# A ninth slot for the gathered v rows, paid for with a norm weight that TensorE spreads

## The chip, the cores and the metric

The kernel runs on one core of one Trainium2 chip. The metric is the device time in microseconds from launch to end; lower is better. A core has TensorE (PE), VectorE (DVE), ScalarE (ACT), GpSimd (POOL) and the queue engine SyncE (SP), each with its own instruction stream, run in order, and 16 DMA engines that all queues share. SBUF and PSUM have 128 partitions.

## What is computed

One layer of a trunk over 1024 tokens of width 1024, in float32: a mixer (latent attention, a gated linear recurrence, differential attention), a cross attention to 256 memory tokens, and an expert layer, then a last norm. The part that moves most bytes is the expert layer. For every token it picks 128 of 16384 experts (8 heads, 16 each); every expert has a row `u` and a row `v` of 1024 numbers:

```python
def peer_ffn(h, w_q, keys, u, v):          # h = rmsnorm(x, norm_ffn)
    ...
    def block(args):
        xt, et, gt = args
        act = jax.nn.gelu(jnp.einsum('td,thkd->thk', xt, u[et]), approximate=False)
        return jnp.einsum('thk,thkd->td', gt * act, v[et])
```

## The kernel before, in words

The tokens go in 8 blocks of 128, one token to a partition. Each block has a front (norm, projections, both attentions, recurrence, cross attention, top-k of the experts) and then its expert rows. The expert rows of block b are worked off while the front of block b+1 runs, so that each engine's stream interleaves two things: pieces of the front, and "positions" p = 0 to 127 of the rows. Tables written out by hand (`TENSOR_STOPS`, `VECTOR_STOPS`, `SCALAR_STOPS`) say for each front piece up to which position the engine has to go before it runs that piece. After block 7's front only rows are left. Block 0's front has no rows beside it.

**Rows.** POOL gathers one row of `u` or `v` for each of the 128 tokens with one indirect DMA of 512 KB (`gather_u`, line 792; `gather_v`, line 802). Its order is fixed: u row i, then v row i-12 (`GATHER_LAG`), then u row i+1, and so on. Both kinds have a ring of `G_RING` = 8 slots, and before each gather POOL waits until the slot's last row was used, so that one gather that has to wait holds up all behind it. DVE multiplies u row p with the normed tokens `h_cur` (line 1986) and counts `u_used`. ACT and DVE turn the products into coefficients; ACT writes them to a diagonal (line 1466). Of v rows, PE multiplies seven of eight with that diagonal and sums in the PSUM tile `ps_sum` (line 1212, 13 positions behind, `v_used`); every eighth (`on_vector`) is added by DVE into `x_cur` (line 2007, `v_added`). Row j lies in slot j % 8, so the DVE's rows always use slot 7, and counters `SUM_SLOTS` = 7 and one credit of `v_added` stand for the free slots of the two readers.

With eight slots, v row i-12 waits for v row i-20, which PE reaches at its position i-7; u row i waits for u row i-8, at DVE's position i-8.

**The norm of the experts.** At the end of a block's front `hand_ids` (line 1950) makes `h_cur` out of `x_next`, the row's scale and the weights `norm_ffn`. The weights lie in SBUF as `ffn_row`, 128 equal copies of one line of 1024 numbers (4 KB of each partition), loaded once at the start by a DMA of 512 KB, the last of the constants on SP's queue.

**The score banks.** `ps_s` is a PSUM tile of two banks that many pieces share. In `peer_scores` PE writes two sets of key scores to it, and ACT copies each out (line 1252, `k_out`) before the next may be written. From there until `latents` of the following block nobody uses `ps_s`.

## Time and profile before

| | |
|---|---|
| median of 3 runs | 3508.47 us (3501.45 to 3508.81) |
| the profiled execution, its own time | 3502.22 us |
| its span, first to last instruction | 3500.1 us |
| PE, DVE, ACT, POOL busy | 84%, 67%, 23%, 57% |
| mean rate of DMA over the span | 385 GB/s |
| span of block 0's front without rows | about 0 to 313 us |
| last block, rows only | about 3152 us to the end |

Busy time of an engine is a share of the whole span; waits are put down to what ended them. "DMA busy" of a stretch is the mean over the 16 engines. A PE in this profile is busy from issue to a modelled end, and one float32 matmul is listed as two instructions.

### The profile page before, as it was taken

To read this page: it belongs to the slowest core of one execution; us is meant where nothing else is said; L and a number is where in the kernel's file an instruction comes from. 1 tells how busy PE (TensorE), PEld (TensorE's weight loads), DVE (VectorE), ACT (ScalarE), POOL (GpSimd) and SP (SyncE) were. 2 spreads that over 40 slices of the span, in tenths; PEclk is the share of its full clock that TensorE was granted. 3 is DMA by queue.
4 is the path that set the end of the run, shared out by engine and by line. 5 is a ranking of instruction groups with operands and counts; after the bars stand their busy time and mean duration, and the time that the engine had idled before them with its cause. 6 is when DMAs were issued, how large, how long until landed. Compare 5 with 4: busy or idle time off the path is not lost.

```text
span 3500.1 us, 34723 instructions
## 1 busy us (share of the span) xinstructions
PE 2942.9 (84%) x10960; PEld 1660.0 (47%) x10960; DVE 2341.0 (67%) x5884; ACT 814.6 (23%) x1924; POOL 2008.2 (57%) x2085
## 2 busy tenths in 40 slices
PE   7786898888997899888987799888998789976777
PEld 6465355533554355444554445544554445522222
DVE  6229756886578765887477855786648866596554
ACT  3111421133111422133211332114221232211111
POOL 1003765666565664666555655666547655577775
PEclk9897999999999999999999999999999999998999
DMA  7787999999999999999999999999999999999998
GB/s 275 259 299 266 409 409 409 408 409 402 409 402 408 399 405 403 407 409 390 405 409 408 397 351 409 409 408 370 354 409 409 409 346 350 390 404 410 409 409 339
DMA packets 387256, 1346.12 MB, mean 385 GB/s; under 512 B 41793, under 2 KB 44865, under 8 KB 386433
## 3 DMA queue, kind: packets, MB, share of 16 engines
q0 software_dynamic: 294912, 1073.87, 78.0%
q1 hardware_dynamic: 91008, 265.83, 20.1%
q10 hardware_dynamic: 1152, 4.19, 0.3%
q8 instruction: 89, 1.46, 0.2%
q14 instruction: 95, 0.77, 0.1%
HBM read 1334.03 MB, written 35.39 MB: 391 GB/s over the span
## 4 chain that ended last, share of the span: by engine, by line
PE 43%; DMA 25%; DVE 14%; POOL 9%; issue 6%; ACT 3%; SPq 0%; DVEq 0%; ACTq 0%; POOLq 0%
PE ps_sum L1212 19%; DMA rows<-in_peer_u,ids_u 9%; PE ps_p L979 7%; DMA rows<-in_peer_v,ids_v 6%; DMA rows<-in_peer_v,ids_u 5%; POOL rows L802 5%; PE ps_s L1127 5%; POOL rows L792 4%; DVE rows L1986 4%; DMA w_ring<-packed 2%; PE ps_s L1065 2%; PE ps_p L1073 2%; DVE feat_b L1873 1%; PE ps_p L1047 1%; DVE feat_b L1869 1%
## 5 line engine op out<-in xcount | busy, mean ns | idle before, releaser
L1212 PE MATMUL ps_sum<-rows,diag 128*128 128x512 f32 x3584 | 1748.0, 631 | 271.9 <-DMA rows<-in_peer_v,ids_v 129.2
L1986 DVE CUSTOM_DVE_ANT_0 rows<-h_cur,rows 128x1024 f32<-128x1024 f32 x1024 | 1228.1, 1220 | 539.7 <-DMA rows<-in_peer_u,ids_u 527.0
L792 POOL DMA_INDIRECT rows<-in_peer_u,ids_u x1024 | 1005.4, 982 | 720.7 <-issue 498.8
L1212 PEld LDWEIGHTS ps_sum<-rows,diag 128*128 128x128 f32 x3584 | 684.1, 201 | 1166.4 <-issue 1047.8
L802 POOL DMA_INDIRECT rows<-in_peer_v,ids_v x512 | 493.5, 964 | 452.2 <-PE ps_sum L1212 295.6
L802 POOL DMA_INDIRECT rows<-in_peer_v,ids_u x512 | 494.4, 966 | 267.8 <-issue 127.3
L1466 ACT ACTIVATE diag<-ident,acts 128x128 f32<-128x128 f32 x896 | 327.4, 394 | 1057.4 <-PE ps_sum L1212 757.5
L979 PE MATMUL ps_p<-hT,w_ring 128*128 128x128 f32 x2944 | 367.8, 286 | 36.1 <-DMA w_ring<-packed 18.0
L979 PEld LDWEIGHTS ps_p<-hT,w_ring 128*128 128x128 f32 x2944 | 362.0, 202 | 68.6 <-issue 42.3
L1772 DVE CUSTOM_DVE_ANT_0 e<-ps_s,bias_t 128x256 f32<-128x256 f32 (+6 forms) x96 | 74.2, 773 | 177.5 <-PE ps_s L1065 70.6
L2007 DVE SCALAR_TENSOR_TENSOR x_cur<-rows,acts,x_cur 128x1024 f32<-128x1024 f32 x128 | 164.0, 1282 | 13.4 <-DMA rows<-in_peer_v,ids_v 13.4
L1843 DVE TENSOR_TENSOR x_next<-x_next,ps_s 128x512 f32<-128x512 f32 x32 | 21.9, 685 | 189.8 <-PE ps_s L1127 189.8
L1454 ACT ACTIVATE acts<-dots 128x8 f32<-128x8 f32 x128 | 26.6, 207 | 453.2 <-DVE dots L1986 453.0
L1127 PE MATMUL ps_s<-w_ring,hT 128*128 128x512 f32 x256 | 117.7, 606 | 12.7 <-DVE hT L1833 6.8
L1379 ACT ACTIVATE e<-e,small 128x256 f32<-128x256 f32 (+6 forms) x96 | 75.4, 786 | 220.6 <-DVE small L1774 220.2
L979 PE MATMUL ps_p<-pT,w_ring 128*128 128x128 f32 x1024 | 118.6, 276 | 1.2 <-DMA w_ring<-packed 0.6
L979 PEld LDWEIGHTS ps_p<-pT,w_ring 128*128 128x128 f32 x1024 | 116.8, 192 | 5.6 <-issue 3.3
L1127 PE MATMUL ps_s<-w_ring,feat_b 128*128 128x512 f32 x256 | 115.4, 594 | 1.1 <-ACT feat_b L1252 0.7
L1065 PE MATMUL ps_s<-k_diff,feat_a 32*128 32x512 f32 (+2 forms) x192 | 84.2, 545 | 24.9 <-DVE small L1774 24.7
L1873 DVE FIND_INDEX8 feat_b<-feat_b,e 128x8 uint32<-128x128 f32 (+1 forms) x384 | 103.4, 279 | 0.0
L1252 ACT ACTIVATE feat_a<-ps_p 128x512 f32<-128x512 f32 (+2 forms) x48 | 26.0, 541 | 317.5 <-PE ps_p L979 317.4
L1986 DVE DVE_READ_ACCUMULATOR2_ANT dots<- 128x1 f32 x1024 | 84.5, 83 | 0.0
(280 smaller groups left out, 2325.7 us busy)
## 6 DMA issues: line engine op xcount, KB each, us to landing
w_ring<-packed SPq DMA_DIRECT2D x343, 512.0 KB, 7.7
w_ring<-in_wstream SPq DMA_DIRECT2D x65, 512.0 KB, 5.3
packed<-in_wstream SPq DMA_DIRECT2D x49, 512.0 KB, 7.9
rows<-in_peer_u,ids_u POOLq DMA_INDIRECT x1024, 13.3
rows<-in_peer_v,ids_u POOLq DMA_INDIRECT x512, 10.7
rows<-in_peer_v,ids_v POOLq DMA_INDIRECT x512, 15.4
bias_rows<-rows SPq DMA_DIRECT2D x5, 1024.0 KB, 12.8
bias_t<-in_x SPq DMA_DIRECT2D x8, 512.0 KB, 6.2
```

The lines of the kernel that those rows point to most:

```text
L792: pool.indirect_dma_start(u_rows[:, j % G_RING, :], None, peer_u, bass.IndirectOffsetOnAxis(ap=ids_u[:, j:j + 1], axis=0)).then_inc(u_land ...
L802: pool.indirect_dma_start(v_rows[:, j % G_RING, :], None, peer_v, bass.IndirectOffsetOnAxis(ap=ids[:, j:j + 1], axis=0)).then_inc(v_landed ...
L979: ins = pe.matmul(dst, w[:, k, :], lhs[:, kt, :], start=(kt == 0), stop=(kt == KT - 1))
L1065: ins = pe.matmul(ps_s[:, c0:c1], q_diff[r:r + DK, half // 4, :], k_diff[r:r + DK, half // 4, c0:c1], start=True, stop=True)
L1127: pe.matmul(ps_s[:, n * 512:(n + 1) * 512], lhs[:, kt, :], w, start=(kt == 0), stop=(kt == KT - 1)).then_inc(w_used, 1)
L1212: ins = pe.matmul(ps_sum[:, c * 512:(c + 1) * 512], diag[:, n % 4, :], v_rows[:, j % G_RING, c * 512:(c + 1) * 512], start=(n == 0), stop= ...
L1379: act.activation(buf[:, 0:keys_n], buf[:, 0:keys_n], ACT.Exp, bias=small[:, 32 + n:33 + n], accum_out=small[:, 48 + n:49 + n]).then_inc(s_ ...
L1466: act.activation(diag[:, n % 4, :], ident[:, :], ACT.Copy, scale=coef[:, j:j + 1]).then_inc(diag_made, 1)
L1772: run(dve.tensor_tensor_reduce(buf[:, 0:keys_n], ps_s[:, 0:keys_n], bias[:, 0:keys_n], 1.0, -3.0e38, ALU.add, ALU.max, small[:, 16 + n:17 ...
L1873: dve.max_index(i[:, first:first + 8], v[:, first:first + 8], s).then_inc(top_step, 1)
L1986: dve.tensor_tensor_reduce(row, h_cur[:, :], row, 1.0, 0.0, ALU.mult, ALU.add, dots[:, p:p + 1]).then_inc(u_used, 1)
L2007: dve.scalar_tensor_tensor(x_cur[:, :], v_rows[:, j % G_RING, :], coef[:, j:j + 1], x_cur[:, :], ALU.mult, ALU.add)\
```

## The change

The ring of v rows gets a ninth slot; that of u rows keeps eight. Rows of all blocks are counted through, and v row j of block b lies in slot (128 b + j) % 9. So the slot of a DVE row moves around the ring, and `gather_v` waits for whoever used the row nine before, by a count that is computed for each row. The slot takes the 4 KB of each partition that `ffn_row` had. The weights are now one line of 4 KB in partition 96 under `k_mla`, which uses partitions 0 to 95, and `spread_ffn` lets PE multiply it with a line of ones into `ps_s`, two matmuls per block of one row of weights by 512 columns each. It runs at the start of the piece `next_norm` in blocks 0 to 6 and right behind `peer_scores` in block 7. PE waits for ACT's second copy out of `ps_s` before it, DVE waits for it in `hand_ids` and reads the weights from PSUM, and `latents` of the next block waits until DVE has read them. The order of the pieces and the stops are the same.

```diff
-G_RING = 8
+U_RING = 8
+V_RING = 9
...
-SUM_SLOTS = G_RING - G_RING // SHARE
+SUM_SLOTS = 7
+ADD_SLOTS = 1
...
-        ffn_row = sb("ffn_row", [P, D])
...
-        k_mla = sb("k_mla", [NOPE + ROPE, MLA_H, SEQ])
+        k_lines = sb("k_lines", [P, MLA_H, SEQ])
+        k_mla = k_lines[0:NOPE + ROPE, :, :]
+        ffn_line = k_lines[96:97, 0, :]
...
-            sp.dma_start(ffn_row[:, :], ffn_gain.partition_broadcast(P)).then_inc(consts_in, 16)
+            sp.dma_start(ffn_line, ffn_gain.partition_broadcast(1)).then_inc(consts_in, 16)
...
+            def gather_v(b, j):
+
+                slot = row_slot(b, j, V_RING)
+                before = b * EXPERTS + j - V_RING
+                if before >= 0:
+                    added = before // SHARE + (1 if on_vector(before % EXPERTS) else 0)
+                    if on_vector(before % EXPERTS):
+                        pool.wait_ge(v_added, ADD_SLOTS + added)
+                    else:
+                        pool.wait_ge(v_used, SUM_SLOTS + before + 1 - added)
...
+            def spread_ffn(b):
+                if isinstance(b, int) and b == 0:
+                    pe.wait_ge(consts_in, 96)
+                pe.wait_ge(k_out, 2 * b + 2)
+                for c in range(2):
+                    ins = pe.matmul(ps_s[:, c * HALF:(c + 1) * HALF], ones[96:97, :], ffn_line[:, c * HALF:(c + 1) * HALF],
+                                    start=True, stop=True)
+                ins.then_inc(ffn_spread, 1)
+
+            def later_norm(b):
+                spread_ffn(b)
+                turn_scaled(b + 1)
+
+            def last_scores(b):
+                peer_scores(b)
+                spread_ffn(b)
+
             def latents(b):
                 pe.wait_ge(lat_sq, b + 1)
+                ge(pe, handed, b)
...
+                dve.wait_ge(ffn_spread, b + 1)
-                dve.scalar_tensor_tensor(h_cur[:, :], x_next[:, :], small[:, 105:106], ffn_row[:, :], ALU.mult, ALU.mult)\
+                dve.scalar_tensor_tensor(h_cur[:, :], x_next[:, :], small[:, 105:106], ps_s[:, :], ALU.mult, ALU.mult)\
                    .then_inc(handed, 1)
```

## Rows read from the trace of the kernel before

**Rows 1.** page, slices of 87.5 us: mean DMA busy tenths, GB/s moved.

```profile
DMA  7787999999999999999999999999999999999998
GB/s 275 259 299 266 409 409 409 408 409 402 409 402 408 399 405 403 407 409 390 405 409 408 397 351 409 409 408 370 354 409 409 409 346 350 390 404 410 409 409 339
```

**Rows 2.** page, DMA queues: packets, MB, share of 16 engines.

```profile
q0 software_dynamic: 294912, 1073.87, 78.0%
```

**Rows 3.** page, groups: busy us, mean ns of one | idle before, releaser.

```profile
L1212 PE MATMUL ps_sum<-rows,diag 128*128 128x512 f32 x3584 | 1748.0, 631 | 271.9 <-DMA rows<-in_peer_v,ids_v 129.2
L1986 DVE CUSTOM_DVE_ANT_0 rows<-h_cur,rows 128x1024 f32<-128x1024 f32 x1024 | 1228.1, 1220 | 539.7 <-DMA rows<-in_peer_u,ids_u 527.0
L792 POOL DMA_INDIRECT rows<-in_peer_u,ids_u x1024 | 1005.4, 982 | 720.7 <-issue 498.8
...
L802 POOL DMA_INDIRECT rows<-in_peer_v,ids_v x512 | 493.5, 964 | 452.2 <-PE ps_sum L1212 295.6
```

**Rows 4.** waits of the whole run: us, times, longest.

```profile
POOL rows L802 <- PE ps_sum L1212: 419.5, 209, 13.3
...
POOL rows L792 <- DVE dots L1986: 221.6, 171, 20.8
```

**Rows 5.** stretches: length, busy us of PE, PEld, DVE, ACT, POOL, clock, DMA, GB/s.

```profile
811.00:823.00 12.00, 12.00 (x35) 5.33 (x33) 5.38 (x16) 5.11 (x11) 8.52 (x10) 0.99 0.97 360
...
989.00:999.00 10.00, 10.00 (x25) 4.46 (x24) 9.71 (x47) 2.05 (x7) 7.52 (x9) 1.00 0.97 358
...
1213.00:1253.00 40.00, 39.02 (x124) 18.50 (x123) 31.27 (x82) 17.47 (x40) 28.47 (x30) 1.00 1.01 386
...
1391.00:1401.00 10.00, 10.00 (x24) 4.37 (x23) 9.72 (x50) 2.00 (x6) 7.56 (x9) 1.00 0.98 351
...
1609.00:1679.00 70.00, 66.03 (x207) 32.66 (x206) 43.22 (x102) 23.90 (x53) 43.19 (x44) 1.00 1.00 380
...
2005.00:2081.00 76.00, 70.86 (x235) 36.83 (x236) 47.97 (x108) 26.73 (x55) 44.99 (x47) 0.96 0.91 330
...
2411.00:2513.00 102.00, 94.40 (x318) 49.09 (x319) 60.67 (x130) 35.27 (x69) 54.91 (x56) 0.97 0.91 328
...
2829.00:2941.00 112.00, 101.72 (x349) 52.44 (x348) 65.79 (x136) 37.85 (x70) 55.71 (x58) 0.97 0.87 314
...
3049.00:3063.00 14.00, 13.68 (x36) 6.95 (x37) 12.23 (x58) 4.09 (x10) 7.85 (x9) 1.00 0.82 286
```

**Rows 6.** waits within 2829 to 2941 us.

```profile
POOL rows L802 <- PE ps_sum L1212: 29.4, 12, 5.9
```

**Rows 7.** timeline of POOL: start, us, instruction [idle before <- releaser].

```profile
2087.20 0.94 POOL L792 DMA_INDIRECT rows<-in_peer_u,ids_u  x1 [7.97 <-DVE dots L1986]
...
2506.99 0.93 POOL L792 DMA_INDIRECT rows<-in_peer_u,ids_u  x1 [8.00 <-DVE dots L1986]
```

**Rows 8.** one microsecond of the stretch after 2506.99, columns of rows 5.

```profile
2510.00:2511.00 1.00, 1.00 (x4) 0.53 (x3) 0.00 (x0) 0.00 (x0) 0.69 (x2) 1.00 0.75 291
```

**Rows 9.** timeline of the last block's PE, ACT and POOL.

```profile
3049.32 1.97 PE L1182 MATMUL ps_s<-keys,feat_a 128*128 128x256 f32 x8 [1.36 <-ACT e L1252]
3051.12 17.33 PE L1212 MATMUL ps_sum<-rows,diag 128*128 128x512 f32 x40
...
3051.33 1.11 ACT L1252 ACTIVATE e<-ps_s,small 128x1024 f32<-128x1024 f32 x1 [2.15 <-PE ps_s L1182]
...
3053.28 0.94 POOL L802 DMA_INDIRECT rows<-in_peer_v,ids_v  x1 [3.93 <-PE ps_sum L1212]
```

**Rows 10.** timeline of PE, same place one of the earlier blocks.

```profile
1006.41 1.97 PE L956 MATMUL ps_p<-ident,feat_a 128*128 128x128 f32 x8 [3.91 <-DVE feat_a L1662]
```

**Rows 11.** groups of DVE: one reading no PSUM, one reading PSUM.

```profile
L1950 DVE SCALAR_TENSOR_TENSOR h_cur<-x_next,small,ffn_row 128x1024 f32<-128x1024 f32 x8 | 10.3, 1285 | 0.0
...
L2025 DVE TENSOR_TENSOR x_cur<-x_cur,ps_sum 128x1024 f32<-128x1024 f32 x1 | 1.2, 1221 | 2.9 <-PE ps_sum L1212 2.9
```

**Rows 12.** chain that ended last, first 40 us: start, us, what.

```profile
15.59 7.90 DMA w_ring<-in_wstream
```

More of the change, by code:

```diff
@@ L292, in sem @@
             return ctx.enter_context(nc.semaphore(name))
-        rows = sb("rows", [P, 2 * G_RING, D])
-        u_rows, v_rows = rows[:, 0:G_RING, :], rows[:, G_RING:2 * G_RING, :]
+        rows = sb("rows", [P, U_RING + V_RING, D])
+        u_rows, v_rows = rows[:, 0:U_RING, :], rows[:, U_RING:U_RING + V_RING, :]
         w_ring = sb("w_ring", [P, W_RING, 2 * HALF])
@@ L434, in program @@
         x_copied, gain_landed = sem("x_copied"), sem("gain_landed")
+        ffn_spread = sem("ffn_spread")
         x_handed, ids_handed, v_ids_handed = sem("x_handed"), sem("ids_handed"), sem("v_ids_handed")
-        u_landed = [sem(f"u_landed{i}") for i in range(G_RING)]
-        v_landed = [sem(f"v_landed{i}") for i in range(G_RING)]
+        u_landed = [sem(f"u_landed{i}") for i in range(U_RING)]
+        v_landed = [sem(f"v_landed{i}") for i in range(V_RING)]
         u_used, v_used = sem("u_used"), sem("v_used")
@@ L545, in row_of, with row_slot, row_landings @@
             return (bp, None) if isinstance(bp, int) and bp == 0 else (bp - 1, j + EXPERTS)
+        def row_slot(b, j, ring):
+            return (b * EXPERTS + j) % ring
+        def row_landings(b, j, ring):
+            return 16 * ((b * EXPERTS + j) // ring + 1)
         def ends_block(bp, p, at):
@@ L891, in _ @@
             for k in range(GATHER_LAG):
-                gather_u(k)
+                gather_u(0, k)
             for b in range(NB):
-                retrieve(more=b < NB - 1)
+                retrieve(b, more=b < NB - 1)
         @block.tensor
@@ L1195, in _ @@
                 front[f"next_{g}"] = lambda b, g=g, first=first, n=n: project(b + 1, g, first, n)
-            front["next_norm"] = lambda b: turn_scaled(b + 1)
+            front["next_norm"] = later_norm
             for h in range(4):
@@ L1206, in add_row @@
                     pe.wait_ge(diag_made, bp * SUM_ROWS + n + 1)
-                    pe.wait_ge(v_landed[j % G_RING], bp * (16 * EXPERTS // G_RING) + 16 * (j // G_RING + 1))
+                    slot = row_slot(bp, j, V_RING)
+                    pe.wait_ge(v_landed[slot], row_landings(bp, j, V_RING))
                     if j == 0:
@@ L1211, in add_row @@
                     for c in range(2):
[L1212 removed]
+                        ins = pe.matmul(ps_sum[:, c * 512:(c + 1) * 512], diag[:, n % 4, :], v_rows[:, slot, c * 512:(c + 1) * 512],
                                         start=(n == 0), stop=(n == SUM_ROWS - 1), skip_group_check=True)
@@ L1239, in _ @@
             for pace.body, (first, last, wide[0]) in enumerate(LOOPS):
+                if first == NB - 1:
+                    front["peer_scores"] = last_scores
                 with pe.Fori(first, last) as b:
@@ L1982, in multiply_row @@
             def multiply_row(bp, p):
-                dve.wait_ge(u_landed[p % G_RING], bp * (16 * EXPERTS // G_RING) + 16 * (p // G_RING + 1))
-                row = u_rows[:, p % G_RING, :]
+                slot = row_slot(bp, p, U_RING)
+                dve.wait_ge(u_landed[slot], row_landings(bp, p, U_RING))
+                row = u_rows[:, slot, :]
                 dve.tensor_tensor_reduce(row, h_cur[:, :], row, 1.0, 0.0, ALU.mult, ALU.add, dots[:, p:p + 1]).then_inc(u_used, 1)
@@ L2001, in position @@
                 if j is not None and on_vector(j):
-                    dve.wait_ge(v_landed[j % G_RING], at * (16 * EXPERTS // G_RING) + 16 * (j // G_RING + 1))
-                    dve.wait_ge(v_added, at * (EXPERTS // SHARE) + (j + G_RING) // SHARE)
+                    slot = row_slot(at, j, V_RING)
+                    dve.wait_ge(v_landed[slot], row_landings(at, j, V_RING))
+                    dve.wait_ge(v_added, at * (EXPERTS // SHARE) + j // SHARE + ADD_SLOTS)
                     dve.wait_ge(coef_made, at * STEPS + (j // STEP + 1))
-                    dve.scalar_tensor_tensor(x_cur[:, :], v_rows[:, j % G_RING, :], coef[:, j:j + 1], x_cur[:, :], ALU.mult, ALU.add)\
+                    dve.scalar_tensor_tensor(x_cur[:, :], v_rows[:, slot, :], coef[:, j:j + 1], x_cur[:, :], ALU.mult, ALU.add)\
                        .then_inc(v_added, 1)
```

41 lines of the change are left out of this document (18 added, 23 removed).

## The prediction, as it was put on record

> **What bounds the kernel now.** I read the page's slices first. From 350 us on the DMA row stands at 9 in every slice but the last, which is an 8, and most slices move 409 GB/s; several move less, down to 346 [rows 1]. So 409 GB/s is the full rate here. 2048 gathers move 1073.87 MB [rows 2], 0.524 MB each, which at 409 GB/s is 1.28 us, and a pair (one u, one v) is 2.56 us. The groups say the same from the other side: DVE's u rows wait 527 us for their gathers, PE's v rows 129 us for one of their two kinds alone [rows 3]. The kernel is bound by DMA wherever the rate is 409, and a change that leaves the bytes alone can only win back time in which the rate is lower. (409 less the rate) / 409 times 87.5 us, added over the 36 slices from 350 us on, is 94 us; 15 us of it are the last slice, where at last nothing is left to load. So 79 us are open.
>
> Next, who holds the gathers up. POOL waits 419.5 us for PE's use of v rows and 221.6 us for DVE's use of u rows [rows 4]. Most of that is harmless, because gathers already issued keep the queues full. It costs only where they run out, so I cut the run into stretches by rate [rows 5]. The loss of each is its length times its shortfall: 1.4 us (811), 1.3 (989), 2.3 (1213), 1.4 (1391), 5.0 (1609), 14.7 (2005), 20.2 (2411), 26.0 (2829), 4.2 (3049). That is 76.5 us, so these nine stretches hold nearly all of it. PE is busy for 91 to 100% of each. In the three wide ones (blocks with many key tiles) PE is busy 93%, 93% and 91%, and the largest wait of POOL is for PE's v rows, 29.4 us within 2829 to 2941 [rows 6].
>
> **The change part by part.**
>
> The ninth slot. POOL may now issue v row i-12 when PE is through position i-8, where it had to be through i-7. POOL therefore runs at most one pair ahead of where it ran: a credit of 2.56 us of DMA work, paid once each time the queues would run dry, if u's ring lets the u row through. It is not paid per wait. Where PE is the limit for a whole stretch, PE's end does not move: the DMA idles a pair less and that is kept only if DMA is the limit again before the next thing that holds POOL. So:
>
> - Short, light stretches (811, 989, 1213, 1391): each loses less than a pair, and rows wait for DMA soon after. All of it is won: 1.4 + 1.3 + 2.3 + 1.4 = 6.4 us. Bounds 3 us (a v slot alone, 1.28 us at most for each, some not kept) and 6.4.
> - 1609, 2005, 2411, 2829: behind each comes a wait of POOL for DVE's u rows, 7.97 and 8.00 us long in two of them [rows 7]. A ninth v slot does nothing there, since u's ring is as it was: POOL stands at the same u row until the same moment. If the queues empty meanwhile, the credit is gone. At 2510 us, behind the wait that ended at 2506.99, the rate is 291 GB/s [rows 8], so the queues had run thin there. I take 1 us each for 1609 and 2005, 0 for the other two; bounds 0 and 2.56 each, 0 to 10.2 in all.
> - 3049, in the last block: below.
>
> The Trainium skill ("Perfetto Trace Analysis", section Optimization Strategy) says that a gap that repeats on the engine that ought to be full can mean too few buffers for the next tile. By that rule all 76.5 us would be the ring's to give back; the trace agrees that the gaps repeat, but not that they are of one kind, since PE is the busy engine in the long ones [rows 5].
>
> The spread. Two matmuls of 512 columns are four listed instructions; v rows of the same columns run at 17.33 / 40 = 0.43 us each [rows 9], so 1.74 us of PE a block. Matmuls with a single row of weights are not in the trace; bounds are 1.0 us (four at 1.97 / 8 = 0.25 us, of half the columns [rows 9]) and 2.5 us (four at the page's mean of 631 ns [rows 3]); 0.43 us is nearest, being of the same columns and type and back to back. In blocks 0 to 6 it stands at `next_norm`, position 93, long after ACT's copy, and v rows wait behind it on PE. Its cover is PE's wait for DVE's scaled x, 3.91 us before the transposes at 1006.41 [rows 10]; the v rows between are 1.74 us late, less than the new lead of a pair. I take 0; without the cover it is 1.74 us in each.
>
> In block 7 there is no cover. It follows `peer_scores` at once, and must wait for ACT's copy, which runs from 3051.33 for 1.11 us, to 3052.44. Before, PE started v rows at 3051.12 [rows 9], and POOL, 3.93 us in waiting, issued its next v gather at 3053.28, on the first of them. Now v rows start at 3052.44 + 1.74 = 3054.2, so 3.1 us late, and POOL's lead is 2.56 us. The two cancel: +0.5 us. Bounds: -2.6 (the spread hides) and +3.1.
>
> DVE reads the weights from PSUM in `hand_ids`: 1285 ns now without a PSUM source, and 1221 ns for an add of the same size with one [rows 11]. Nothing, within 0.1 us eight times. The Trainium skill ("Perfetto Trace Analysis", section Optimizing Scalar/DVE Operations) gives some 125 ns of access overhead for PSUM against 60 for SBUF, an estimate of 0.5 us over the eight; the rows show none of it, and the sum would be -8.4 us by it. The new waits: DVE's for the spread comes some 30 positions after it; PE's in `latents` is covered by its wait for squares that DVE makes only behind `hand_ids`. Both 0. The u rows, the POOL instruction count and the gathers' order are unchanged: 0.
>
> The load. 512 KB become 4 KB, 1.28 us less on SP's queue, ahead of the fifth weight load, whose 7.90 us are in the chain of waits [rows 12]. Block 0 has no gathers to hide it. I take 1.0 us; bounds 0 and 1.3.
>
> Sum: -6.4 - 2.0 + 0.5 - 1.0 = -8.9 us. The profiled execution took 3502.22 us itself (span 3500.1), so 3493.3 us. The shown median is 3508.47, 6 us above that execution; a saving of waits is the same from either, so the predicted median is 3499.6 us.
>
> **The rivals.**
>
> *Every bubble pays.* The stretches are not one bound each: the wide ones have full patches inside, and where the queues fill up again between two PE pieces the pair is credited anew. With a full pair in 1609, 2005, 2411, 2829 and 3049, and two to three in the wide ones, that is 6.4 + 2 x 2.56 + 3 x 2.5 x 2.56 + 1.3 = 32 us at most, 3476; with one in each, 6.4 + 5 x 2.56 + 1.3 = 20.5 us, 3488. For it: several POOL waits for PE in each, 12 in the last [rows 6]. Against it: PE is busy above 90% there, and the waits for DVE behind. The rule of the Trainium skill on repeating gaps ("Perfetto Trace Analysis", Optimization Strategy) speaks for this rival.
>
> *Nothing is kept.* DVE's u ring holds POOL next, and the pair only moves the dry spot: 0 to -3 us, 3505 to 3508. For it: 221.6 us of waits for DVE [rows 4] that nothing here touches, and the lead needs a u row through as well. Against it: rows wait for DMA directly behind the light stretches.
>
> *The spread decides, slower.* If PE is what POOL waits for with dry queues when the spread comes, all of it is on the path: 7 x 1.74 + 3.1 = 15.3 us, less 2 us of start and light stretches, 3522. It decides once the v rows behind the spread come more than a pair, 2.56 us, late. That holds in block 7 (3.1 us); in the others only if the spread costs near its upper bound and something else is late as well, such as DVE's scaled x, so that PE's 3.91 us are gone.
>
> **How the numbers follow.** My forecast (4 to 13 us less) 0.53; every bubble pays 0.17; nothing is kept 0.20; the spread decides 0.10. Time 3499.6 us. The range must leave out two tenths at most: down to half of the first rival, 3485, and up past the second, to 3511; the forecast's own range is 3495 to 3504. 0.2% is 7 us, about what a measurement of this kernel can tell from none. Faster by more: six tenths of the forecast and all of the first rival, 0.50. Within: the rest of the forecast and most of the second, 0.40. Slower: 0.10.
>
> **What would show it.** Right: POOL's wait for PE's v rows falls well below 419.5 us; stretches below 409 GB/s vanish in the light blocks and stay in the wide ones, followed by the same 8 us for DVE; two matmuls into `ps_s` before the last block's v rows with some 1.3 us of wait for ACT; the other seven with no wait for ACT and PE still idle before the transposes behind them; the bytes less by 0.52 MB. It would be wrong if the wide stretches' losses of 61 us fall by more than a quarter, if a v row late behind the spread shows up as a dry queue in each block, or if DVE comes to wait more for u rows than now because v gathers stand ahead of them.

## The result, and the profile after

| | before | after |
|---|---|---|
| median of 20 runs | 3501.48 us | 3509.51 us |
| lowest to highest | 3495.92 to 3508.81 | 3501.32 to 3515.65 |
| the profiled execution's own time, span | 3502.22, 3500.1 | 3510.99, 3509.1 |
| DMA bytes | 1346.12 MB | 1345.62 MB |

The ratio is 1.0017 (95% interval 1.0009 to 1.0024): 6 us slower by the ratio and 8 by the medians, where the prediction had 9 us faster. That is inside the 0.2% that I had called no change, but on the other side of zero. In a second comparison (below) the ratio was 1.0005 (0.9996 to 1.0013), which isn't clear of no change. Slower by 2 to 8 us is the reading, and the 9 us that were forecast are out of reach of both intervals.

From the page of the changed kernel: the slices of GB/s, and the groups of v rows, u rows and gathers (they answer to [rows 1, 3]):

```profile
GB/s 268 266 291 275 409 409 409 408 409 406 409 406 408 382 405 409 409 409 372 391 409 408 408 344 410 409 409 377 347 409 409 409 343 351 382 403 397 410 409 346
...
L1249 PE MATMUL ps_sum<-rows,diag 128*128 128x512 f32 x3584 | 1750.2, 631 | 288.5 <-DMA rows<-in_peer_v,ids_v 144.7
L2027 DVE CUSTOM_DVE_ANT_0 rows<-h_cur,rows 128x1024 f32<-128x1024 f32 x1024 | 1228.7, 1221 | 550.7 <-DMA rows<-in_peer_u,ids_u 538.6
L805 POOL DMA_INDIRECT rows<-in_peer_u,ids_u x1024 | 1013.9, 990 | 860.2 <-issue 486.2
...
L819 POOL DMA_INDIRECT rows<-in_peer_v,ids_v x512 | 490.6, 958 | 355.5 <-PE ps_sum L1249 229.6
```

POOL's waits in the changed kernel (they answer to [rows 4]):

```profile
POOL rows L805 <- DVE dots L2027: 374.0, 206, 21.4
POOL rows L819 <- PE ps_sum L1249: 306.8, 207, 11.1
```

What the reader is to see: the forecast of one view came true, POOL waits less for PE (419.5 to 306.8 us). But it waits as much more for DVE (221.6 to 374.0), and DVE in its turn waits no less for its u rows (527.0 us before, 538.6 now). The hold went from one ring to the other.

The page also has the median time of a gather from its issue to its landing (last number). Before:

```profile
rows<-in_peer_u,ids_u POOLq DMA_INDIRECT x1024, 13.3
...
rows<-in_peer_v,ids_v POOLq DMA_INDIRECT x512, 15.4
```

and after:

```profile
rows<-in_peer_u,ids_u POOLq DMA_INDIRECT x1024, 13.9
...
rows<-in_peer_v,ids_v POOLq DMA_INDIRECT x512, 18.0
```

A v gather may now be issued up to 2.56 us earlier, and half of them (those by `ids_v`) take 2.6 us longer to land; the other half takes 0.6 us longer (10.7 to 11.3), and so do the u gathers. For the first half, then, the lead went into waiting between issue and landing. This repeats in the experiments below, on the chips of 3503 to 3507 us: 17.8 to 18.2 us in all eight profiles with nine v and eight u slots, 15.3 to 16.4 in all four with eight and eight, and for u rows 13.7 to 13.9 against 12.9 to 13.3.

Next, the blocks. DVE makes `h_cur` once a block, so I cut both runs at its starts; the columns are those of [rows 5]. Blocks 2, 3, 4 and the last stretch before the final `h_cur`, of the kernel before:

```profile
701.50:1102.70 401.20, 347.25 (x1293) 193.96 (x1292) 284.45 (x725) 97.25 (x239) 248.61 (x256) 0.94 1.02 406
1102.70:1506.00 403.30, 351.62 (x1317) 198.23 (x1316) 286.95 (x725) 99.26 (x239) 247.39 (x256) 0.95 1.02 405
1506.00:1908.60 402.60, 351.10 (x1365) 202.08 (x1364) 288.33 (x725) 102.27 (x239) 251.17 (x256) 0.97 1.02 404
2741.20:3151.50 410.30, 348.87 (x1171) 181.16 (x1170) 291.31 (x712) 106.89 (x234) 247.59 (x255) 0.96 0.97 378
```

and of the changed kernel:

```profile
700.50:1101.60 401.10, 345.86 (x1297) 193.12 (x1296) 284.37 (x724) 97.53 (x239) 251.33 (x256) 0.95 1.03 408
1101.60:1504.70 403.10, 355.43 (x1321) 198.42 (x1320) 286.72 (x724) 99.61 (x239) 250.13 (x256) 0.94 1.02 402
1504.70:1914.20 409.50, 361.19 (x1369) 207.34 (x1368) 288.33 (x725) 102.69 (x239) 248.04 (x256) 0.95 1.01 397
2746.20:3162.10 415.90, 353.79 (x1176) 183.82 (x1174) 291.88 (x713) 106.90 (x234) 250.56 (x256) 0.95 0.97 376
```

The first `h_cur` starts at 311.9 us (313.3 before) and the changed kernel is 1.0 to 1.4 us ahead up to 1504.7. Blocks 2 and 3 are 401.1 and 403.1 us long, and were 401.2 and 403.3: nothing was won there. Nearly the whole loss lies in block 4 (402.6 to 409.5) and in the last stretch (410.3 to 415.9).

Within blocks 2 to 4 of the changed kernel, the same stretches as in [rows 5]:

```profile
810.00:822.00 12.00, 12.00 (x36) 5.48 (x35) 5.33 (x16) 5.07 (x11) 8.67 (x10) 1.00 1.02 405
988.00:998.00 10.00, 10.00 (x24) 4.15 (x23) 9.72 (x47) 1.82 (x6) 7.56 (x9) 1.00 1.01 395
1180.00:1230.00 50.00, 44.26 (x140) 21.54 (x138) 31.33 (x68) 19.08 (x47) 32.65 (x35) 0.86 0.98 367
1390.00:1400.00 10.00, 10.00 (x24) 4.05 (x23) 9.72 (x49) 2.11 (x6) 7.50 (x8) 1.00 1.03 408
1590.00:1600.00 10.00, 9.75 (x27) 5.68 (x27) 6.01 (x13) 4.74 (x9) 7.13 (x9) 0.66 1.03 409
```

and of the kernel before, the two that answer to 1180 and to 1590:

```profile
1182.00:1232.00 50.00, 44.28 (x144) 21.60 (x142) 34.32 (x74) 19.39 (x47) 33.64 (x36) 0.93 1.01 392
1591.00:1601.00 10.00, 9.31 (x35) 5.13 (x36) 8.39 (x17) 5.72 (x11) 7.30 (x9) 1.00 1.02 406
```

811, 989 and 1391 are full now (losses 0.1, 0.3 and 0.0 us, by the method of the prediction). But 1180 to 1230 loses 50 x 42 / 409 = 5.1 us where the kernel before lost 50 x 17 / 409 = 2.1. Sum of the four: 5.6 us, and it was 6.2 to 6.4. The 1213 stretch itself (1211 to 1251 here) moves 370 GB/s for 386, so it did not fill. In block 4 the clock was granted at 0.66 from 1590 to 1600 us, where the kernel before had it whole, and the rate over the 20 us behind it is 357 for 395. The wide stretches, cut at the same distance from `h_cur` (2010 to 2086, 2418 to 2520, 2834 to 2946), lose 10.6, 18.5 and 26.6 us (14.7, 20.2 and 26.0 before), and the one of 1609 (1608 to 1678 here) loses 9.9 for 5.0.

The last block's PE, and POOL's next v gather behind it (they answer to [rows 9]):

```profile
3054.77 1.97 PE L1218 MATMUL ps_s<-keys,feat_a 128*128 128x256 f32 x8 [1.36 <-ACT e L1291]
3057.94 2.62 PE L1024 MATMUL ps_s<-k_lines,ones 1*128 1x512 f32 x4 [1.20 <-ACT e L1291]
3060.48 15.86 PE L1249 MATMUL ps_sum<-rows,diag 128*128 128x512 f32 x30
```

```profile
3064.54 0.94 POOL L819 DMA_INDIRECT rows<-in_peer_v,ids_v  x1 [9.76 <-PE ps_sum L1249]
```

From the second scores to the v rows it is 60.48 - 54.77 = 5.71 us, and was 51.12 - 49.32 = 1.80 [rows 9]: 3.9 us late. POOL stands 9.76 us, and stood 3.93. A timeline row of POOL in block 5 shows what became of the wait of 7.97 us [rows 7]:

```profile
2092.05 0.94 POOL L805 DMA_INDIRECT rows<-in_peer_u,ids_u  x1 [9.17 <-DVE dots L2027]
```

### The profile page after: what moved, and what is told of

It is laid out like the page before. It is cut to its first block, busy times and chain, and to the rows that moved or that the text cites. A ratio compares the mean times of both kernels' runs of the same rounds, so it can differ in the third digit from the quotient of the medians.

```text
span 3509.1 us, 34795 instructions
## 1 busy us (share of the span) xinstructions
PE 2958.0 (84%) x10992; PEld 1663.2 (47%) x10992; DVE 2342.0 (67%) x5884; ACT 816.8 (23%) x1924; POOL 2024.2 (58%) x2085
## 2 busy tenths in 40 slices
DMA packets 387114, 1345.62 MB, mean 383 GB/s; under 512 B 41777, under 2 KB 44849, under 8 KB 386290
## 4 chain that ended last, share of the span: by engine, by line
PE 39%; DMA 29%; DVE 13%; POOL 9%; issue 6%; ACT 3%; SPq 0%; DVEq 0%; ACTq 0%
PE ps_sum L1249 18%; DMA rows<-in_peer_u,ids_u 14%; DMA rows<-in_peer_v,ids_v 7%; PE ps_p L996 6%; POOL rows L805 5%; POOL rows L819 5%; PE ps_s L1163 4%; DMA rows<-in_peer_v,ids_u 4%; DVE rows L2027 4%; DMA w_ring<-packed 2%; PE ps_s L1101 2%; PE ps_p L1109 2%; DVE feat_b L1912 1%; PE ps_p L1083 1%; PE ps_s L1097 1%
## 5 line engine op out<-in xcount | busy, mean ns | idle before, releaser
L1249 PE MATMUL ps_sum<-rows,diag 128*128 128x512 f32 x3584 | 1750.2, 631 | 288.5 <-DMA rows<-in_peer_v,ids_v 144.7
L2027 DVE CUSTOM_DVE_ANT_0 rows<-h_cur,rows 128x1024 f32<-128x1024 f32 x1024 | 1228.7, 1221 | 550.7 <-DMA rows<-in_peer_u,ids_u 538.6
L819 POOL DMA_INDIRECT rows<-in_peer_v,ids_u x512 | 504.8, 986 | 216.5 <-issue 137.2
L2049 DVE SCALAR_TENSOR_TENSOR x_cur<-rows,acts,x_cur 128x1024 f32<-128x1024 f32 x128 | 164.1, 1282 | 13.9 <-DMA rows<-in_peer_v,ids_v 13.9
L1493 ACT ACTIVATE acts<-dots 128x8 f32<-128x8 f32 x128 | 26.6, 208 | 469.2 <-DVE dots L2027 469.0
## 6 DMA issues: line engine op xcount, KB each, us to landing
rows<-in_peer_u,ids_u POOLq DMA_INDIRECT x1024, 13.9
rows<-in_peer_v,ids_u POOLq DMA_INDIRECT x512, 11.3
```

The source lines that it names most:

```text
L819: pool.indirect_dma_start(v_rows[:, slot, :], None, peer_v, bass.IndirectOffsetOnAxis(ap=ids[:, j:j + 1], axis=0)).then_inc(v_landed[slot] ...
L1249: ins = pe.matmul(ps_sum[:, c * 512:(c + 1) * 512], diag[:, n % 4, :], v_rows[:, slot, c * 512:(c + 1) * 512], start=(n == 0), stop=(n == ...
L2027: dve.tensor_tensor_reduce(row, h_cur[:, :], row, 1.0, 0.0, ALU.mult, ALU.add, dots[:, p:p + 1]).then_inc(u_used, 1)
L2049: dve.scalar_tensor_tensor(x_cur[:, :], v_rows[:, slot, :], coef[:, j:j + 1], x_cur[:, :], ALU.mult, ALU.add)\
```

## The experiments

Times are given as the ratio to the kernel before in runs on the same chip. The chips differ: the kernel before took 3503 to 3507 us on the two of the runs e1 to e4, f and g, and 3730 (e5 to e8) and 3715 us (h) on the two others. The slots are for u and v rows; "early" is the last block's spread at position 89 as in the change, "late" is at 93.

| run | slots u, v | last spread | ratio | interval |
|---|---|---|---|---|
| the change | 8, 9 | early | 1.0017 | 1.0009 to 1.0024 |
| e1_spread_only | 8, 8 | early | 1.0013 | 1.0002 to 1.0025 |
| e2_ring_only | 8, 9 | none | 1.0009 | 0.9997 to 1.0020 |
| e3_late_spread | 8, 9 | late | 0.9992 | 0.9979 to 1.0006 |
| e4_spread_in_wait | 8, 9 | late, others moved | 1.0010 | 0.9999 to 1.0021 |
| f1_eight_late | 8, 8 | late | 0.9991 | 0.9980 to 1.0002 |
| f2_full_rows | 8, 9 | early, 128 rows | 1.0004 | 0.9993 to 1.0015 |
| f3_changed_again | 8, 9 | early | 1.0005 | 0.9996 to 1.0013 |
| f4_nine_late | 8, 9 | late | 1.0000 | 0.9990 to 1.0010 |
| g1_nine_nine | 9, 9 | late | 0.9958 | 0.9944 to 0.9971 |
| g2_nine_u | 9, 8 | late | 0.9972 | 0.9959 to 0.9984 |
| g3_eight_late | 8, 8 | late | 0.9981 | 0.9970 to 0.9991 |
| g4_nine_late | 8, 9 | late | 0.9991 | 0.9980 to 1.0002 |
| on the chips of 3715 to 3730 us | | | | |
| e5_eight_late | 8, 8 | late | 0.9982 | 0.9946 to 1.0017 |
| e6_full_rows | 8, 9 | early, 128 rows | 1.0150 | 1.0100 to 1.0199 |
| e7_nine_u | 9, 8 | late | 1.0048 | 1.0017 to 1.0078 |
| e8_late_again | 8, 9 | late | 1.0141 | 1.0092 to 1.0189 |
| h1_nine_u | 9, 8 | late | 1.0043 | 1.0019 to 1.0067 |
| h2_nine_u_early | 9, 8 | early | 1.0064 | 1.0035 to 1.0093 |

### The two halves of the change apart

The spread without the slot:

```diff
-V_RING = 9
+V_RING = 8
```

> Eight slots for v rows again; the line, its spread by TensorE and the load of 4 KB stay. Theory A, the spread is what costs: in the last block v rows come 3.3 us late without a slot's lead to cover it, elsewhere 2.6 us of PE seven times is partly on the path; the ratio to the kernel before is 1.002 or more (+8 us or more), and the ring had only given back 1 to 6 us of it. Theory B, the ninth slot is what costs (POOL's hold passes from PE's v rows to DVE's u rows): the spread costs its 3.3 us in the last block less 1 us of the smaller load, +1 to +3 us, ratio 1.0003 to 1.0009. In the profile: A sees shortfalls of the rate near positions 93 of each block that the kernel before has not; B sees them only in the last block.

The slot without the spread:

```diff
-            sp.dma_start(ffn_line, ffn_gain.partition_broadcast(1)).then_inc(consts_in, 16)
+            sp.dma_start(gain_row[:, :], ffn_gain.partition_broadcast(P)).then_inc(consts_in, 16)
...
-            sp.dma_start(gain_row[:, :], final_gain.partition_broadcast(P)).then_inc(gain_landed, 16)
+            sp.dma_start(ffn_line, final_gain.partition_broadcast(1)).then_inc(gain_landed, 16)
...
-                spread_ffn(b)
...
-                dve.wait_ge(ffn_spread, b + 1)
-                dve.scalar_tensor_tensor(h_cur[:, :], ..., ps_s[:, :], ALU.mult, ALU.mult)
+                dve.scalar_tensor_tensor(h_cur[:, :], ..., gain_row[:, :], ALU.mult, ALU.mult)
```

> Nine slots for v rows and no spread: the experts' weights lie spread over the partitions in the buffer of the final norm's weights, and the final norm is scaled by them too (this changes the output of the final norm); of the bytes, the 4 KB and the 512 KB loads change places. Theory A, the spread is what costs: the ring's saving is seen alone, 3 to 9 us below the kernel before, ratio 0.9975 to 0.999. Theory B, the ninth slot is what costs: 4 to 8 us above the kernel before, ratio 1.001 to 1.0023, with POOL's waits for DVE's u rows some 150 us more than before and those for PE 110 us less, and the fourth block (1475 to 1884 us) several us longer. Theory C, the ring is worth nothing and the two small costs of the spread add up: within 1 us of the kernel before.

Neither half is faster than the kernel before: +0.13% and +0.09% (the second interval reaches zero). The theories can't be told apart by these totals: the first interval holds both A and B, and of the second only A, the saving of 3 to 9 us, is outside. The executions of one kernel scatter by some 6 us either way; the profiles say more than the totals do, below.

### The last block

```diff
-                    front["peer_scores"] = last_scores
+                    front["top_0"] = spread_ffn        # with "top_0": (93,) in the last TENSOR_STOPS
```

> The changed kernel, but in the last block the spread stands four positions later, at position 93 in place of 89, when ACT's copy is done and v rows have been run. Theory A: the 3.3 us that v rows came late (and the fall of the clock behind them) are gone: 3 us less than the changed kernel, ratio to the kernel before about 1.0013. Theory B: the same 3 us at most, the rest of the loss stays, since it comes from the slot. A reading of no difference to the changed kernel would say that POOL's lead covered the late v rows.

The same kernel three times more:

> The nine-slot kernel with the spread of the last block at position 93 once more, to narrow its ratio (0.9992, 0.9979 to 1.0006 the first time). If the late v rows and the fall of the clock behind the early spread are the changed kernel's loss, it stands 5 to 9 us under the changed kernel again, at 0.998 to 1.000 of the kernel before; if the first reading was chance, at 1.001 to 1.002. In the profile, no fall of the clock within 10 us behind the last spread, and a loss under 3 us behind the last block's scores, where the changed kernel has 7.3.

> Nine slots and the late spread in the last block, beside the changed kernel on one chip. On a chip like the first: 5 to 9 us less than the changed kernel, 0.998 to 1.000 of the kernel before. On a chip like the second: the same as the changed kernel within 5 us, since there it is the slot that costs some 57 us.

> Eight u and nine v slots with the late spread: 0.999 to 1.001 of the kernel before on a chip like the first (0.9992 and 1.0000 so far), so 1 to 3 us above eight and eight, though the last block alone is 2.6 us better; 1.014 on a chip like the second. The prediction had 9 us less than eight slots.

And with eight slots for v rows (`V_RING = 8`), three times:

> Eight slots for v rows, the spread in the last block at position 93 (the pair to the run of late spread with nine slots, and to the run of spread only). So far the spread at 89 cost 5 to 8 us in the last block with either ring, of which 3.3 us are late v rows and the rest a fall of TensorE's clock right behind it. Theory 1, that is all there is to the loss: without it this kernel is within 2 us of the kernel before (ratio 0.9995 to 1.0005), and the last block's granted clock shows no fall within 10 us behind the spread. Theory 2, the spreads of the other blocks cost too: 3 us or more above the kernel before. What the nine-slot kernel with the late spread has less than this one is the ring's worth: 6 to 9 us by the prediction, 0 by the theory that the hold only passes to DVE's u rows.

> Eight slots and the spread of the last block at position 93 again: the last comparison fell on a chip on which the kernel before itself took 3730 us, with a longer tail of slow DMA packets (one in a hundred over 486 ns, against some 200 ns), so this one is for a chip like the first. If the chip is like the first: within 2 us of the kernel before by the theory that only the last block's spread costs; 3 us or more above it if the other spreads cost too. The nine-slot kernel of the same call less this one is the ring's worth: 0 by the theory of the hold that passes to DVE, 6 to 9 us less by the prediction.

> Eight and eight with the late spread, the third time: 0.9985 to 1.0 of the kernel before on any chip (0.9991 and 0.9982 so far), by the smaller load at the start and nothing else.

Then the spread early again, with 128 rows:

```diff
-                spread_ffn(b)
+                pe.wait_ge(k_out, 2 * b + 2)
+                for c in range(2):
+                    ins = pe.matmul(ps_s[:, c * HALF:(c + 1) * HALF], ones[:, :], mem_v[:, 0, c * HALF:(c + 1) * HALF],
+                                    start=True, stop=True)
+                ins.then_inc(ffn_spread, 1)
```

> The changed kernel with the spread of the last block at position 89 as it is, but its two matmuls read 128 rows (all ones times a part of the cross attention's values) in place of one, so the last block's u rows are multiplied by other weights than the reference's. Theory 1, matmuls of one row count as idle time for TensorE's clock: no fall of the clock directly behind it, each matmul takes some 433 ns like a v row's in place of 588, and the kernel is 2 to 4 us faster than the changed one (ratio to the kernel before 1.0005 to 1.001). Theory 2, it is the 1.2 us of waiting for ACT and the late rows that count: the clock falls here too, and the time is that of the changed kernel, ratio 1.0015 to 1.002.

> The changed kernel with 128 rows in place of one in the last block's two matmuls of the spread (so the last block's u rows meet other weights than the reference's) again. The theory that matmuls of one row count as idle time for the clock: no fall of the granted clock within 10 us behind them, as in its first run, and 2 to 4 us less than the changed kernel of this call. The theory that the wait and the late rows cost: the same time as the changed kernel.

The change itself again:

> The changed kernel itself again, beside the three variants on one chip. On a chip like the first: 1.001 to 1.0024 of the kernel before. If its last spread is the cause, the profile again has the clock at half for about 6.8 us from 1 to 2 us behind that spread and a loss of 6 to 10 us there; if the fall was chance, it is not there. The fourth block (seven us longer in the first profile, with three falls of the clock in its attention) tells whether that was chance: 402 us if so, 409 if not. On a chip like the second, both nine-slot variants took 1.5% more, and this one should too: 1.013 to 1.018.

The view that settles this block is the 25 us from the start of the second scores, one row for each kernel, columns as in [rows 5]. Before (eight slots, no spread):

```profile
3049.32:3074.32 25.00, 23.01 (x56) 10.36 (x56) 21.16 (x83) 5.92 (x14) 16.19 (x18) 1.00 0.91 340
```

The change (nine slots, early):

```profile
3054.77:3079.77 25.00, 23.80 (x51) 10.62 (x52) 17.71 (x78) 5.12 (x12) 11.43 (x14) 0.86 0.79 289
```

Spread only (eight slots, early):

```profile
3052.86:3077.86 25.00, 23.80 (x51) 10.64 (x52) 16.94 (x78) 5.11 (x12) 11.32 (x14) 0.86 0.66 244
```

Ring only (nine slots, no spread):

```profile
3058.35:3083.35 25.00, 24.52 (x60) 11.23 (x60) 22.45 (x85) 5.92 (x14) 16.23 (x18) 1.00 1.00 387
```

The first run with the late spread (nine slots):

```profile
3047.22:3072.22 25.00, 25.00 (x62) 11.58 (x63) 22.25 (x85) 5.92 (x14) 16.22 (x18) 1.00 1.00 383
```

The third run with eight slots and the late spread:

```profile
3053.45:3078.45 25.00, 24.67 (x60) 11.14 (x60) 21.64 (x84) 5.92 (x14) 16.16 (x17) 1.00 0.89 341
```

Nine slots, early, 128 rows (the f2 run):

```profile
3057.41:3082.41 25.00, 23.80 (x59) 11.20 (x60) 20.66 (x83) 5.92 (x14) 13.61 (x16) 1.00 0.88 328
```

Loss is 25 x (409 - rate) / 409 us:

| v slots | no spread | late | early, 128 rows | early |
|---|---|---|---|---|
| eight | 4.2 | 3.9, 4.2 | | 10.1 |
| nine | 1.3 | 1.6, 1.3, 2.0, 1.8 | 5.0 | 7.3, 7.6 |

Every cell fits a sum of three prices, to a few tenths. The slot gives 2.4 to 2.9 us (the pair was 2.56). The late spread costs nothing. The early one costs 5.8 to 6.0 us: 3.3 of it with 128 rows already, the late v rows. The other 2.5 come with the clock, 0.86 in all three early runs with one row and 1.00 in every other of the table.

A stretch that moves more bytes need not end sooner, so I took the time as well, from the start of the second scores to the block's `h_cur`: 102.2 to 103.0 us with eight v slots and no or a late spread, 99.5 to 100.8 with nine; early, 109.1 with eight and 107.0 and 107.3 with nine, and 104.3 with 128 rows. The differences are the same three prices: 2 to 3 us for the slot, none for the late spread, 6 to 7 for the early one, of which some 4 stay with 128 rows.

The totals are less clear. The f2 run was to be 2 to 4 us faster than the change on the same chip, and it is 1.0004 against 1.0005; the late spread with nine slots (f4) was to be 5 to 9 us faster, and it is 1.0000, some 2 us. So the price of the early spread, and the part of it that is clock, are read from this stretch alone and not confirmed by a total. On the slow chip e8_late_again, which was to lose under 3 us in the stretch, lost 5.5.

PE's rows of the f2 run, where the two matmuls stood in the same place behind the same wait for ACT:

```profile
3057.41 1.97 PE L1222 MATMUL ps_s<-keys,feat_a 128*128 128x256 f32 x8 [1.36 <-ACT e L1295]
3060.57 1.98 PE L1036 MATMUL ps_s<-mem_v,ones 128*128 128x512 f32 x4 [1.20 <-ACT e L1295]
3062.40 13.90 PE L1253 MATMUL ps_sum<-rows,diag 128*128 128x512 f32 x32
```

From the scores to the v rows 4.99 us, so 3.2 us late. Its clock was whole; in the change, it stood at half from 3059.2 us for 6.8 us, and again so, 1.3 us behind the spread's start, in the second profile of the change. So behind matmuls of one row beside a wait the clock fell, and behind those of 128 rows it did not. With one row this is three profiles of three on the chips of 3505 us, with 128 rows one, so it is likely rather than proven. On the chip of 3715 us the early one-row spread of h2_nine_u_early had no such fall, against what was expected of it; its v rows were 3.3 us late and its stretch lost 6.9 us, where the late spread of h1_nine_u lost 3.7. That is the price of late v rows without the clock's.

### The other seven spreads

The run of late spread, and `pace.part(0.6)` ahead of the spread in `later_norm` (position 99 for 93):

> As the run before it, and in the other seven blocks the spread stands directly ahead of the wait for DVE's scaled x (position 99 in place of 93), so it lies wholly in time in which PE waits. Theory A, the spread's 2.6 us of PE hold v rows up in each block: up to 7 times 1.7 to 2.6 us less than the run before it, so at or below the kernel before, ratio 0.996 to 1.000. Theory B, the slot costs: no difference to the run before it, within 1.5 us.

The change has the spread of block 2 and the transposes behind it so:

```profile
991.04 1.98 PE L1024 MATMUL ps_s<-k_lines,ones 1*128 1x512 f32 x4
992.95 10.57 PE L1249 MATMUL ps_sum<-rows,diag 128*128 128x512 f32 x24
1005.60 1.10 PE L973 MATMUL ps_p<-ident,feat_a 128*128 128x128 f32 x8 [2.09 <-DVE feat_a L1701]
```

The spread holds PE 1.91 us. PE's wait for DVE's scaled x is down from 3.91 us [rows 10] to 2.09, and the eight transposes take 1.10 us for 1.97, since the clock no longer falls there: in blocks 1 to 6 it fell to half at the transposes or within 1.5 us of their start in six of six before (in two only behind them), in none of six now. In the second profile of the change it fell in two of six, behind waits of 3.84 and 5.52 us. Moved into the wait, in block 5, the spread left this:

```profile
2217.03 1.98 PE L1025 MATMUL ps_s<-k_lines,ones 1*128 1x512 f32 x4
2220.62 1.93 PE L974 MATMUL ps_p<-ident,feat_a 128*128 128x128 f32 x8 [1.61 <-DVE feat_a L1701]
```

with this clock in the six microseconds at the transposes (columns as in [rows 5]):

```profile
2220.00:2226.00 6.00, 5.38 (x15) 3.39 (x16) 5.24 (x9) 0.40 (x1) 4.78 (x5) 0.72 1.03 410
```

where the run of late spread has

```profile
2221.00:2227.00 6.00, 5.56 (x19) 3.04 (x20) 5.46 (x9) 0.80 (x2) 4.70 (x5) 1.00 1.03 409
```

The clock fell so in five of the six blocks, with the wait itself down to 1.15 to 1.8 us in four of them: here, too, matmuls of one row next to a wait did not hold the clock up. It cost no length of a block, since the rate is 409 there, and the total (1.0010 against 0.9992) can't tell: the two intervals overlap. The theory that the seven spreads hold v rows up has nothing for it: out of their way, they gave no gain.

### Which ring

Nine slots for u rows and eight for v rows, with the late spread:

```diff
-U_RING = 8
-V_RING = 9
+U_RING = 9
+V_RING = 8
```

> The late spread with the ninth slot in the ring of u rows (nine for u, eight for v). Theory H, in the changed kernel POOL's hold passed from PE's v rows to DVE's u rows, so that either ring alone only moves it: POOL waits some 370 to 420 us for PE's v rows again and under 150 us for DVE's u rows, and the time is that of the eight-slot kernel with the late spread within 2 us. Theory U, the waits for DVE are the ones that end with dry queues in the wide stretches (2411, 2829): 3 to 8 us less than with eight and eight. The prediction's account (PE is the busy engine there) says no gain.

> Nine slots for u rows, eight for v rows, late spread. Theory P: no gain over eight and eight, one ring alone only moves the wait. Theory Q: no gain either; a loss on a chip like the second (1.0048 there). A gain of 3 us or more over eight and eight would say that u was the ring that mattered. POOL's waits for DVE's u rows should fall below 150 us and those for PE stay above 350.

> Nine u slots, eight v slots, the last block's spread at position 93, again. The theory that what is late is DVE's u row, so that only the ring of u pays: 0.996 to 0.9985 of the kernel before, DVE's waits for u rows near 480 us (before 527), and the first whole block some 3 us shorter. If the first reading was chance: 0.998 to 1.000, as eight and eight.

The same with the early spread:

> The changed kernel with its ninth slot in the other ring: nine u slots, eight v slots, the last block's spread at position 89. If slot and spread are separate costs: 5.8 us above the run before it, with a loss of about 10 us behind the last block's scores (that is the loss with eight v slots and the early spread; 7.5 with nine) and the clock at half for some 6.8 us there; ratio to the kernel before 0.998 to 1.000.

Nine in both rings; `gain_row` makes the room, and the final norm takes `mem_v[:, 0, :]` in its place:

> Nine slots in both rings, with the late spread; the room comes from the final norm's weights, which are left out (the final norm is scaled by a part of the cross attention's values instead, so its output differs, and 508 KB less are loaded, 1.2 us of DMA). Theory P, the lead needs a slot in both rings: the light stretches' 6.4 us and the wide ones' 2 us are won on top of the last block's 2.6, ratio 0.997 to 0.998. Theory Q, gathers in flight are not what the blocks wait for: no more than the 1.2 us of the load and the 2.6 us of the last block under eight and eight, ratio 0.998 to 1.0005 on a chip like the first, and more than 1.005 on a chip like the second.

On the chip of g1 to g4 the u slot is the one that pays: 0.9972, and with both 0.9958, of which 0.0004 is the load that is left out. Eight and eight with the late spread is at 0.9981 there, so most of 0.9972 is not the slot's: 3 us are by the ratios, 5 by the medians (3499.19 to 3494.39), from six executions of g2_nine_u; the two intervals overlap. On the two slower chips the same kernel lost (1.0048 and 1.0043), where 0.996 to 0.9985 had been expected of h1_nine_u. The waits of POOL and DVE in g2_nine_u:

```profile
POOL rows L820 <- PE ps_sum L1246: 496.6, 249, 12.9
...
POOL rows L806 <- DVE dots L2024: 120.5, 142, 19.5
```

```profile
DVE rows L2024 <- DMA rows<-in_peer_u,ids_u: 480.9, 309, 3.9
```

the same wait of DVE in g3_eight_late, the kernel with eight and eight on the same chip:

```profile
DVE rows L2024 <- DMA rows<-in_peer_u,ids_u: 510.6, 322, 4.2
```

and blocks 1 and 2 and the last stretch of g2_nine_u, cut at `h_cur`:

```profile
310.20:696.40 386.20, 324.16 (x1230) 186.99 (x1231) 274.70 (x710) 91.16 (x227) 240.67 (x250) 0.93 1.01 399
696.40:1097.70 401.30, 346.63 (x1296) 192.99 (x1295) 284.28 (x725) 97.61 (x239) 247.24 (x256) 0.95 1.02 405
...
2736.20:3143.10 406.90, 352.10 (x1176) 181.52 (x1174) 291.09 (x712) 106.66 (x234) 246.82 (x256) 0.96 0.98 383
```

POOL waits for PE longer than with eight and eight (496.6 us for 432.6 in g3_eight_late and 419.5 before the change), and the kernel is faster all the same. What fell is DVE's wait for u rows: 480.9 us, and 482.0 with nine and nine, where the four profiles with eight and eight have 501.8 to 527.0 and the eight with nine v slots 516.2 to 538.6. Block 1 is 386.2 us (385.6 with nine and nine), and 388.1 to 389.2 in the twelve profiles with eight u slots; the last stretch is 406.9, and was 410.3. Blocks 2 and 3 are 401.3 and 403.0: no ring shortened those, they sum to 803.4 to 804.5 us in all fourteen profiles.

The last row of the last block's table, for this kernel:

```profile
3040.23:3065.23 25.00, 24.39 (x59) 10.97 (x60) 23.10 (x88) 6.03 (x14) 16.17 (x17) 1.00 1.03 408
```

The rate is full, but from these scores to `h_cur` it takes 102.9 us, as with eight and eight: what this kernel gains in the last stretch lies ahead of the scores (304.1 us for 307.6 to 308.1 in three of the four profiles with eight and eight, 315.0 in the fourth).

## Why the prediction was wrong, by its steps

- **What bounds it.** Right in the large: most slices stay at 409 GB/s, and only time below that rate was open. The step that failed comes next: I took POOL's largest wait (419.5 us, for PE's v rows) as the one to shorten.
- **The ninth slot in the light stretches, -6.4 us.** This is the step that made the prediction wrong. Three of the four stretches did fill, as forecast (1213 did not: 370 GB/s for 386); the blocks did not get shorter (804.5 us before, 804.2 now, for blocks 2 and 3). I let the credit of a pair stand although POOL's next wait is for DVE, with the condition "if u's ring lets the u row through" in the text and no price on it. The rival that nothing is kept described it: the dry spot moved (5.6 us of loss for 6.4), and POOL's waits for DVE took over. The v gathers that were issued earlier took longer to land (15.4 to 18.0 us for half of them), and PE waited no less for them (129.2 to 144.7 us). That u rows are the ones that come late is argued from three things: DVE's 527 us stood beside PE's 129 in my own rows [rows 3] (53 more for PE's other kind), these waits fell with nine u slots, and block 1 got 2 to 3 us shorter with those alone. One of the signs that I had named for being wrong came: DVE waits more for u rows than before (538.6 us), but 11 us is within what kernels of the same rings differ by (501.8 to 527.0).
- **1609 and 2005, -1 us each.** Not won: the 1609 stretch loses more (9.9 us for 5.0), and the 2005 one less (10.6 for 14.7), but its block is 413.4 us for 412.1. 2411 and 2829, 0, were right. The waits for DVE behind 2005 and 2411 are 9.17 and 8.94 us (7.97 and 8.00 before).
- **The spread hidden in blocks 0 to 6.** Right: 1.91 us of PE (1.74 forecast), and the wait takes it.
- **The last block, +0.5 us.** Its mechanism was right and both its terms held: v rows 3.2 us late with the clock whole (3.1), the slot worth 2.6 (2.56). A third term was missing, 2.5 us of clock. Measured: 7.3 - 4.2 = +3.1, the upper bound.
- **`h_cur` from PSUM, 0.** Right; no access overhead of the order that the Trainium skill gives ("Perfetto Trace Analysis", section Optimizing Scalar/DVE Operations) can be seen. The group in the changed kernel, 1281 ns for 1285:

```profile
L1990 DVE SCALAR_TENSOR_TENSOR h_cur<-x_next,small,ps_s x8: 1276/1281/1281, 311.9 to 3162.1; 128x1024 f32<-128x1024 f32 x8
```

- **The load, -1.0 us (0 to -1.3).** Probably mis-sized. The first `h_cur` starts at 313.3 and 313.4 us in the two kernels that spread 512 KB at the start; in the twelve profiles with the line outside the slower chips at 307.6 to 313.6, mean 309.8. (The largest is a profile of the change itself, so one profile doesn't show it.) So it seems worth some 3.6 us, more than its own transfer; that is an estimate from two profiles against twelve that scatter by 6 us, and why it should be more was not tried. It agrees with eight slots and the late spread at 0.9991 and 0.9981.
- **Slower after all.** By these prices the change should come out at -3.6 + 3.1 = -0.5 us, and it was +8.0 and +1.8 (0.05%). So the slot for v rows may cost something beside its 2.6 us gain in the last block. The pairs on one chip point to how much: f4 less f1 is +0.0009, g4 less g3 +0.0010, 3 us each, and near 6 us with the last block's gain taken out; but in both pairs the intervals overlap. Whether and where it is lost isn't settled. A candidate is block 4, 6.9 us longer in the first profile with its clock at half from 1591 us on. Three of eight profiles with nine v slots show that (407.5 to 409.1 us from its first gather to the next block's; the other five 402.0 to 404.0), none of four with eight and eight does (401.6 to 403.5); the second profile of the change doesn't. But such long readings, most at a lower mean clock, come elsewhere and without the ninth slot too: block 6 takes 425.5 to 426.2 us (416.9 to 420.5 otherwise) in three profiles with nine v slots and in g3_eight_late, and the time from the last block's start to its second scores 314.4 to 316.3 us (304.1 to 311.2 otherwise) in three with nine and in e1_spread_only. Counted over these three places it is 9 of 24 readings with nine v slots, 2 of 12 with eight and eight, too few to tell. The same 2.24 us gap of PE stands ahead of it with and without the fall, so what decides is not in these rows.
- **The rival "the spread decides"** had the right sign, but by 7 x 1.74 us that were not on the path. Its deciding point, v rows more than 2.56 us late, was met in the last block alone (3.9 us there; the spread takes 1.91 us in the others).

The Trainium skill's rule on repeating gaps ("Perfetto Trace Analysis", Optimization Strategy: too few buffers for the next tile) is met in part: with nine u slots the runs on the chip of 3507 us agree with it, for 3 to 5 us of the 76.5; with nine v slots no run does, and on the slower chips neither ring does.

**Faster versions.** Nine u slots, eight v slots, the last spread late: 0.9972 of the kernel before on one chip, but 1.0048 and 1.0043 on the two chips of 3730 and 3715 us. Eight and eight with the late spread is below 1 on all three chips that ran it (0.9991, 0.9981, 0.9982), though only one interval stays clear of 1.

## What to carry to other kernels

The longest wait of the engine that issues transfers needn't name the ring that is too short. Ask which landed data an engine stands and waits for, and give the slot to that ring; if issue is in order, a slot elsewhere can just move the hold to the next instruction, and the lead into a longer time to landing. A dry stretch that fills is no gain until the next block boundary comes earlier: cut both traces there. And work placed on TensorE beside a wait should be priced with the clock behind it.

## What the runs showed of the hardware

- The clock fell behind matmuls of one row beside a wait as it did behind a wait: to half for 6.8 us in the last block of three profiles (not in h2_nine_u_early), and at the transposes in five of six blocks of e4_spread_in_wait. The two one-row matmuls took 1.91 us until the next work, the two of 128 rows 60.57 to 62.40, 1.83.
- Two of the four chips of the experiments ran the kernel before in 3730 and 3715 us. There the mean rate is lower in most slices. One in a hundred of the gathers' row packets took over 486 ns in e5_eight_late and 530 in e8_late_again, for 213 before and 199 after on the first chip. GB/s in slices, eight slots for v rows and then nine, both late:

```profile
GB/s 285 259 259 320 353 389 401 391 364 352 409 395 371 335 374 400 381 376 297 404 392 394 344 342 409 404 392 301 350 406 390 387 289 363 390 323 369 374 365 320
```

```profile
GB/s 275 263 254 316 347 381 382 397 347 338 406 387 369 346 364 400 373 363 324 394 391 381 333 317 396 386 382 325 329 398 394 368 289 339 370 339 361 367 377 312
```

There a ninth v slot costs 1.0141 - 0.9982, 1.6%, a ninth u slot 0.7% on that chip, and on the other its kernel is 0.4% above the kernel before. More slots and slower packets stand together in these rows; which makes the other was not tried.
